# A two-layer streaming encoder on one core: the norms' inverse roots move behind the projections, and output projection, FFN and the next input projection share one block

## The reference, cut to what matters

```python
def _rmsnorm(x, g):
    y = xf * lax.rsqrt(jnp.mean(xf * xf, axis=-1, keepdims=True) + EPS)
    return (y * g.astype(jnp.float32)).astype(x.dtype)

def _conv_ffn(h, p, prev):
    a, b = jnp.split(h @ p['w_ffn_up'], 2, axis=-1)
    a_ext = jnp.concatenate([prev.astype(a.dtype), a], axis=1)
    c = p['b_ffn_conv']
    for j in range(CONV_W):
        c = c + a_ext[:, j:j + T] * w[j]
    u = jax.nn.gelu(c) * b
    return u @ p['w_ffn_down'], a_ext[:, T:]

def _layer(x, p, past):
    mix, st = _token_mixers(_rmsnorm(x, p['g_norm1']), p, past)
    x = x + mix
    ffn, conv_state = _conv_ffn(_rmsnorm(x, p['g_norm2']), p, None if past is None else past['ffn_conv'])
    return x + ffn, st + (conv_state,)
```

## Time and profile before

| what | us |
|---|---|
| median of three runs | 3460.55 (3459.49 to 3461.61) |
| span of the profiled execution | 3459.4 |
| head, to the first matmul of the input projection | 75.44 |
| gap ahead of the output projection of layer 0 | 46.95 |
| gap between output projection and FFN of layer 0 | 42.43 |
| FFN of layer 0 (956.23 to 1720.54) | 764.31 |
| gap between the layers | 61.89 |
| end, after the FFN of layer 1 | 32.19 |

### The profile page before, as it was taken

How to read it: one execution, slowest core, us unless ns; L and a number is a source line. 1 busy time by engine, 2 the same in 40 slices (tenths; PEclk the granted TensorE clock), 3 DMA queues, 4 the chain that set the end, 5 groups by cost and what they waited for, 6 DMA issues and landing times. The chain is left out here.

```text
span 3459.4 us, 51015 instructions
## 1 busy us (share of the span) xinstructions
PE 3027.6 (88%) x20158; PEld 2809.3 (81%) x20158; DVE 1529.6 (44%) x2564; ACT 1039.1 (30%) x2252; POOL 745.5 (22%) x348
## 2 busy tenths in 40 slices
PE   5998967686799999999859988776776999999997
PEld 3998845466699999999859976545576999999997
DVE  3306646743334344444333266557423444444442
ACT  4223525543222121222032244454413222122211
POOL 3121142103221122212131121411122212122210
PEclk7999968888999999999979999687788999999998
DMA  4110010002021111111031101000110111111111
GB/s 161 36 51 21 2 47 17 1 8 86 18 61 37 49 49 49 38 47 49 13 104 48 40 22 38 11 17 1 63 37 25 61 37 49 48 49 37 54 42 51
DMA packets 164453, 144.53 MB, mean 42 GB/s; under 512 B 15540, under 2 KB 155356, under 8 KB 163804
## 3 DMA queue, kind: packets, MB, share of 16 engines
q1 hardware_dynamic: 164316, 142.72, 13.0%
HBM read 121.32 MB, written 21.48 MB: 41 GB/s over the span
## 5 line engine op out<-in xcount | busy, mean ns | idle before, releaser
L1672 POOL TENSOR_TENSOR fwlo<-fraw,fwhi 128x1024 fp32r<-128x1024 f32 x132 | 319.9, 2424 | 1160.9 <-ACT fwhi L1744 1152.5
L529 PE MATMUL wps<-whi,h_hi 128*128 128x246 f32 (+1 forms) x1296 | 363.0, 280 | 53.3 <-POOL wlo L490 53.3
L1691 PE MATMUL fpsA<-g_hi,fwhi 128*128 128x352 f32 x1056 | 343.1, 325 | 47.7 <-POOL fwlo L1672 47.7
L1843 DVE TENSOR_TENSOR xT<-xT,fpsD 128x352 f32<-128x352 f32 x528 | 275.3, 521 | 233.8 <-PE fpsD L1705 233.8
L529 PE MATMUL wps<-whi,h_lo 128*128 128x246 f32 (+1 forms) x1296 | 360.7, 278 | 0.0
L529 PE MATMUL wps<-wlo,h_hi 128*128 128x246 f32 (+1 forms) x1296 | 360.7, 278 | 0.0
L1705 PE MATMUL fpsD<-fuhi,fwhi 128*128 128x352 f32 x1056 | 340.2, 322 | 6.6 <-issue 6.6
L1705 PE MATMUL fpsD<-fulo,fwhi 128*128 128x352 f32 x1056 | 341.9, 324 | 0.0
L1705 PE MATMUL fpsD<-fuhi,fwlo 128*128 128x352 f32 x1056 | 340.9, 323 | 0.0
L1691 PE MATMUL fpsB<-g_hi,fwhi 128*128 128x352 f32 x1056 | 340.6, 323 | 0.0
L1691 PE MATMUL fpsA<-g_hi,fwlo 128*128 128x352 f32 x1056 | 340.5, 322 | 0.0
(11 more groups left out here) (377 smaller groups left out, 6330.6 us busy)
## 6 DMA issues: line engine op xcount, KB each, us to landing
fraw<-in_w_ffn_up SPq DMA_DIRECT2D x88, 512.0 KB, 3.8
fraw<-in_w_ffn_down SPq DMA_DIRECT2D x44, 512.0 KB, 3.4
wraw<-in_w_in SPq DMA_DIRECT2D x18, 984.0 KB, 5.2
x_between<-xT SPq DMA_DIRECT2D x2, 4224.0 KB, 13.0
xT<-x_between SPq DMA_DIRECT2D x2, 4224.0 KB, 15.4
oraw<-in_w_out SPq DMA_DIRECT2D x16, 512.0 KB, 4.1
xin<-in_x_prompt SPq DMA_DIRECT2D x8, 512.0 KB, 3.5
out_y_prompt<-xout SPq DMA_DIRECT2D x8, 512.0 KB, 2.6
```

Of the source, the lines that this page charges most:

```text
L529: last = pe.matmul(ps[0:n, t % NB, 0:WN], a[:, c, at], w[:, b, c, :], start=(c == 0 and m == 0), stop=(c == DC - 1 and m == 2))
L1672: pool.tensor_tensor(wlo[:, r], raw[:, o % 2], whi[:, r].bitcast(F32), ALU.subtract)\
L1691: last = pe.matmul(ps[:, t, 0:TN], w[:, role, c, :], x[:, c, at], start=(c == 0 and m == 0), stop=(c == DC - 1 and m == 2))
L1843: last = dve.tensor_tensor(x, x, psD[:, o % 2, 0:TN], ALU.add)
```

## The change

The inverse root leaves the operand. The input projection takes x times gain, split into high and low, and its evacuation multiplies each token's row by the root. In the FFN the gate rows are multiplied by the root when they leave PSUM (DVE), and the gelu's result is multiplied by the root on POOL, ahead of its product with the up rows. The norm as a separate stage stays for the mixers' result alone. What was several blocks becomes one:

- `first_layer_in`: loading, turning, splitting and step 0 of the input projection go token tile by token tile.
- `layer_out`: output projection, FFN, and the next layer's split and first step (layer 0) or the turning and storing of y (layer 1). x is read from DRAM chunk by chunk into two buffers, and written back, in the output projection, and read whole (`load_x`) as the FFN begins. The last pair's down pieces go third by third, and in layer 0 each piece has ACT's high part and square, DVE's low part and POOL's addition of the squares behind it (`Tail`).
- The layers are unrolled; 103 semaphores are cleared ahead of the norm of the mixers' result, in each layer, and none behind norms or FFN.

```diff
-        with nc.Fori(0, DEPTH) as lay:
-            one_layer(nc, k, lay)
+        first_layer_in(nc, k, places, proj, prep[0])
+        for lay in range(DEPTH):
+            y_hi, y_lo, raw = mixers(nc, k, lay, places, proj, prep[lay], layer)
+            layer_out(nc, k, lay, places, y_hi, y_lo, raw, proj, prep[min(lay + 1, DEPTH - 1)])
...
+class ProjectOut:
+    def sync(self, sp, load_next):
+        for m in range(DC):
+            sp.wait_ge(self.lo_w[m % 2], m // 2 + 1)
+            if m + 2 < DC:
+                self.load_w(sp, m + 2)
...
+            sp.wait_ge(self.x_lo, NT * (m + 1))
+            sp.dma_start(self.k.x_dram[:, m, :], self.xs[m % 2][:, :]).then_inc(self.x_out[m % 2], 16)
+            if m + 2 < DC:
+                sp.wait_ge(self.x_out[m % 2], 16 * (m // 2 + 1))
+                self.load_x(sp, m + 2)
...
+    def roots(self, act):
+        for t in range(NT):
+            act.wait_ge(self.summed, t + 1)
+            act.activation(self.rsb[:, self.cols(t)], self.bank[:, 6 + t % 2, 0:TN], ACT.Ln, scale=1.0 / D,
+                           bias=k.const[:, C_EPS:C_EPS + 1]).then_inc(self.logged, 1)
+        act.wait_ge(self.logged, NT)
+        act.activation(self.rsb[:, :], self.rsb[:, :], ACT.Exp, scale=-0.5).then_inc(self.rooted, 1)
...
+class ConvFFN:
+    def scale(self, pool, g, e):
+        pool.wait_ge(self.gelu_done, 2 * g + (e + 1))
+        pool.tensor_tensor(v, v, self.rsb[:, 0:SEQ], ALU.mult)
+        pool.tensor_tensor(w, w, self.rsb[:, SEQ:TOK], ALU.mult).then_inc(self.scaled, 1)
...
+class Tail:
+    def scalar(self, act):
+        for o in range(self.O):
+            self.ffn.added(act, o)
+            act.activation(self.k.hi[:, m, at], x, ACT.Copy, scale=self.gain[:, m:m + 1]).then_inc(self.hi_done, 1)
+            if o >= 2:
+                act.wait_ge(self.squares_added, o - 1)
+            act.activation(self.sq[:, o % 2, :], x, ACT.Square).then_inc(self.squared, 1)
...
+    def low_part(self, dve, o):
+        dve.wait_ge(self.hi_done, o + 1)
+        dve.scalar_tensor_tensor(self.k.lo[:, m, at], self.ffn.xT[:, m, at], self.gain[:, m:m + 1],
+                                 self.k.hi[:, m, at].bitcast(F32), ALU.mult, ALU.subtract).then_inc(self.lo_done, 1)
```

More of the change, by code:

```diff
@@ L146 @@
     pass
[L149 to L205, removed]
@@ L208, in store_tokens @@
[L208 to L247, removed]
@@ L312, in norm @@
+def norm(nc, k, xT, hi, lo, vec, gain, tag, groups, also):
     with ExitStack() as s:
@@ new lines, in _ @@
+                pin.load_first(sp, 0)
+                for t in range(1, TT):
+                    ld.tokens(sp, t)
+                pin.load_first(sp, 1)
+                rows.load(sp)
+                ld.store(sp)
+                pin.load(sp)
+            @block.tensor
+            def _(pe):
+                ld.turn_vectors(pe)
+                pin.tensor(pe, front)
+            @block.scalar
+            def _(act):
+                ld.scalar_first(act)
+                pin.split(act, 0)
+                pin.scalar(act, front)
@@ new lines, in _ @@
+                ffn.load_x(sp)
+                ffn.load(sp)
+                if last:
+                    ffn.store_state(sp)
+                    out.store(sp)
+                    sp.wait_ge(ffn.stored, 32)
+                else:
+                    sp.wait_ge(ffn.b_done, 6 * ffn.PAIRS)
+                    pin.load_first(sp, 0)
+                    pin.load_first(sp, 1)
+                    ffn.store_state(sp)
+                    rows.load(sp)
+                    tail.store(sp)
+                    sp.wait_ge(ffn.stored, 32)
+                    pin.load(sp)
@@ new lines, in _ @@
+            @block.tensor
+            def _(pe):
+                pout.tensor(pe, y_hi, y_lo)
+                if last:
+                    ffn.tensor(pe, lambda third: out.behind(pe, third))
+                else:
+                    ffn.tensor(pe, lambda third: None)
+                    pin.tensor(pe, front)
+            @block.scalar
+            def _(act):
+                pout.high(act, 0)
+                pout.scalar(act, ffn.high_first)
+                ffn.scalar(act)
+                if last:
+                    out.scalar(act)
+                else:
+                    pin.split(act, 0)
+                    tail.scalar(act)
+                    pin.scalar(act, front)
@@ L1860, in restart @@
+                pout.low(pool, 0)
+                pout.pool(pool, ffn.low_first)
+                ffn.pool(pool)
+                if not last:
+                    pin.low(pool, 0, 0)
+                    tail.pool(pool)
+                    pin.pool(pool, 1)
 def restart(nc, sems):
```

1347 lines of the change are left out of this document (871 added, 476 removed).

## The result

The changed kernel took 3336.97 us (3335.93 to 3337.98, four runs), the kernel before 3460.38 on the same chip: ratio 0.9641, interval 0.9628 to 0.9655. It is faster by 123 us, where 162 were forecast. The time lies 5 us above the range given, 3272 to 3332.

A forecast was written before the change was run, and what follows sets the result against it. PE bounds the kernel, busy 88% of the span, so gains come only where it waits. Head -33, output projection to FFN -76, between layers -49, end -19, clears +15 sum to -162: 3298 us, range 3272 to 3332.

The forecast's parts named there:

- The change takes no matmul out of these stretches, so it can gain only where PE waits: Input projection, output projection and FFN: PE never idles there, so gains come only from head, gaps and end.
- At nothing: The FFN's loop: FFN's steady rounds: no change in time, as PE covers POOL's added 2.6 us per chunk.
- the other rivals: Output projection starves, 0.2; better than forecast, 0.11; slower than before, 0.03; no change, 0.02.
- SP's queue starves nothing: Rival, output projection: w_out loads queue on SP behind x's stores, +28 us, 3326; chance 0.2.
- POOL's product holds up nothing: Rival, FFN: POOL's product between gelu and gate makes PE wait in all 44 chunks, 3518 at 5 each; chance 0.03.
- The head: Kernel start, once: first matmul at 22.7, tiles at 4.2, step 0 ends at 60; -33 us, bounds -26 and -40.
- Output projection to FFN: Gap between those products, twice: only 6.7 of 44.8 us stays; -38 each, -76, bounds -43 and -32 each.
- Between the layers: Layer 0's last pair, once: helpers take 1.4 us a piece within the down pieces; -49 us, bounds -57 and -39.
- The end: After the last matmuls, once: seven tiles, a copy and the last store leave 13.2 of 32.19 us; -19, +-4.
- The clears: Ahead of the mixers' result's norm, twice: 103 clears take 8.7 us; +7.5 each, +15, bounds +6 and +9.
- The mixers: Mixers of both layers: stay as they are, change 0.

The follow-up runs named there:

- the aligned kernel: Against the changed kernel, all hand-placed buffers moved to begin at multiples of 32 bytes, nothing else changed: 3295.04 us, ratio to before 0.9522.
- The run without the squares: Against the version with all buffers at multiples of 32 bytes, POOL's additions of squares in layer 0's last pair cut to one column of 352: 3296.14 us.
- the first chunk's order changed: Against the version with buffers at multiples of 32 bytes, second chunk's weights loaded and split ahead of whole x, roots and POOL's root product: 3288.23 us.

## Why the prediction was wrong

**The step that failed** is "The change takes no matmul out of these stretches, so it can gain only where PE waits", and with it "At nothing: The FFN's loop". It took the products' own time as fixed, at 0.159 us a matmul; measured were 0.163. The forecast checked order, waits and helpers for the loop, but not the operands' addresses, which the change sets itself. By the table above the addresses cost 21.6 us between layer 0's output projection and layer 1's mixers, 20.5 from layer 1's output projection on, and 3.4 up to the end of the first input projection; ahead of the output projections the offset gives 2.3 back, through POOL. Without the offset the kernel takes 3295, where 3298 was forecast. That this is so near is in part luck: the aligned kernel's head falls 7 us short of the forecast, and the stretch through layer 0's FFN gains 6.5 more than forecast, the mixers 4 and the end 2. No rival named it, and none of the other rivals happened: the output projections take 95.1 us without idle time, so SP's queue starves nothing, and POOL's product holds up nothing behind the first chunk.

**The head** was mis-sized: -33 forecast, -26 aligned. Its loop left out two steps of DVE, gain and staging copy, 1.23 and 1.22 us for each tile, the first of which stands in the loop: the first matmul came at 26.3 instead of 22.7, tiles at 4.75 instead of 4.2, step 0 ended at 69.1 instead of 60. And the wait of the evacuation for the store, the first tile's evacuation at 35.72 for a store issued at 25.02, wasn't in the sum; without it step 1 starts 4.7 us earlier, of the 7 missing.

**Output projection to FFN** was right, in place and in size: from the output projection's first matmul to the FFN's 1500th the aligned kernel takes 39.0 us less than the kernel before in layer 0 and 39.1 in layer 1, where 38 was forecast. ACT and POOL in the changed kernel, and PE's group with the wait:

```profile
911.11 1.09 ACT L1745 ACTIVATE rsb<-rsb 128x1056 f32<-128x1056 f32 x1
...
917.46 1.09 ACT L2037 ACTIVATE fcb<-fcb 128x1058 f32<-128x1058 f32 x1 [1.98 <-DVE fcb L2104]
```

```profile
918.62 2.41 POOL L1907 TENSOR_TENSOR fcb<-fcb,rsb 128x1024 f32<-128x1024 f32 x1 [17.91 <-ACT fcb L2037]
...
921.20 4.80 POOL L1898 TENSOR_TENSOR fwlo<-raw,fwhi 128x1024 fp32r<-128x1024 f32 x2
```

```profile
L1942 PE MATMUL bank_b<-x_hi,fwhi 128*128 128x352 f32 x68 | 23.7, 349 | 2.6 <-POOL fwlo L1898 2.6
```

Counted from the first matmul at 895.51, the gelu ends at 23.0 (forecast 23.1), POOL's product at 25.7 (25.6), the low part at 28.1 (28.4). B's matmuls end at 25.4 instead of 24.7, so PE waits 2.65 us behind it, where 3.7 was forecast, in both layers; the clock is 0.50 from 924.4 to 927.8. The forecast's sum had a slip: 23.1, 2.5 and 2.42 make 28.0 and not 28.4, and the wait by it would have been 3.3.

**Between the layers** the mechanism was right and the size 1.25 us a piece instead of 1.4. POOL and DVE in layer 0's last pair of the changed kernel:

```profile
1660.15 4.34 POOL L499 TENSOR_TENSOR wlo<-wraw,whi 128x1968 fp32r<-128x1968 f32 x1 [5.92 <-ACT whi L508]
...
1665.35 3.52 POOL L2212 TENSOR_TENSOR rsb<-rsb,sqo 128x352 f32<-128x352 f32 x3
```

```profile
1660.58 4.28 DVE L2194 SCALAR_TENSOR_TENSOR x_lo<-fx,vec,x_hi 128x352 fp32r<-128x352 f32 x1 [1.51 <-ACT x_hi L2186]
...
1665.22 0.58 DVE L2194 SCALAR_TENSOR_TENSOR x_lo<-fx,vec,x_hi 128x352 fp32r<-128x352 f32 x1
...
1666.14 0.83 DVE L2194 SCALAR_TENSOR_TENSOR x_lo<-fx,vec,x_hi 128x352 fp32r<-128x352 f32 x1
```

DVE's low part of 352 columns takes 4.28 us beside POOL's low part of 1968 columns (4.34), 0.58 where POOL does nothing as it begins, and 0.83 beside one of POOL's additions (up to 1.29 in this pair), while DVE's addition with an input in PSUM stays at 0.51 to 0.52. This agrees with the Trainium skill, SBUF — State Buffer, "Who interferes with whom", by which the two engines' reads of SBUF exclude each other for a whole instruction where DVE has two inputs there. The run without the squares shows both ends: 1.25 and 1.05 a piece. The last pair takes 37.1 us from the last up matmul on, forecast 41. Here too the sum had a slip: 41 against 27.9 gives back 13.1 and not 13.6.

**The end**: from the last down matmul at 3320.4 to the span's end 13.4 us; 13.2 forecast. **The clears**: the pause ahead of the norm grew from 4.0 to 11.7 us, 7.7 for 103 where 8.7 was forecast; with what fell away behind the norm the whole stretch grew by 6.2 and 5.6 (forecast 7.5). **The mixers** became 4 us shorter, which I had not forecast and have not traced.

## What to carry to other kernels

When a change places buffers by hand, compute every operand's address by 32 before anything else, and round the base. The allocator that aligned them in the kernel before did work that nobody saw. Compare the spacing of matmuls in a stretch without idle time, before and after: it is the first number to look at when a gain falls short though the waits went as planned. And a wait that is taken out leads to the next one in the same block: here the second chunk's weights on POOL, a store's landing in the head, each worth 3 to 7 us. Effects of this size are near what two executions of one kernel differ by (the aligned one took 3291.87 to 3297.13), so their place is the stretch itself.

## What the runs showed of the hardware

- The start address of TensorE's fp32r operands in SBUF sets part of a matmul's time: with 352 columns, at full clock and without a wait, 0.1591 us at multiples of 32 bytes, 0.1629 with x and the weights at a remainder of 8 and the gelu product at 24, 0.1607 with all at 16. The moving operand counts more than the stationary one (up matmuls with x off alone 0.162, with the weights off alone 0.1605). The Trainium skill, SBUF — State Buffer, "Operand start alignment", asks for a multiple of the element size and says that this is about legality and that its runs timed nothing; all versions here obey it, and differ by 42 us.
- POOL's subtraction of two float32 inputs of 1024 columns takes 2035 ns with one input at a remainder of 8 by 32 and the other at 0, and 2437 to 2441 with both at the same remainder.
- A pause of the same length (2.24 us ahead of layer 1's last pair) was followed by the full clock in one execution (aligned), by 3.4 us at half clock in a second (the first chunk's order changed) and by 6.8 in a third (without the squares). Full clock against 6.8 us at half clock is 2.9 us in the next 96 matmuls.
